# Opening of a two-block transformer kernel: who shifts the first chunk, which split comes first, and the order of the products

## The reference, cut to what matters

```
mods = silu(c) @ w_ada + b_ada            # 9 vectors of 1024: shift, scale, gate, three times
n = rmsnorm(x, g_pre) * (1 + scale) + shift
f = (silu(n @ w_gate) * (n @ w_up)) @ w_down
```

## Time and profile before

| | |
|---|---|
| median of three runs | 1135.86 us |
| the profiled execution | 1135.31 us |
| its span, first to last instruction | 1134.0 us |
| TensorE busy | 1118.3 us, 99% |
| VectorE busy | 821.5 us, 72% |
| ScalarE busy | 637.4 us, 56% |
| GpSimd busy | 56.6 us, 5% |
| granted TensorE clock | 0.999 of full |

### The profile page before, as it was taken

One profiled execution on the slowest core, in us unless ns is written; L12 is line 12 of the kernel. 1 busy time (PEld: TensorE's weight loads), 2 busy tenths in 40 slices (PEclk: granted clock), 3 DMA queues, 4 the chain that ended last, 5 costly groups with the idle time before them and its releaser, 6 DMA issues.

```text
span 1134.0 us, 16844 instructions
## 1 busy us (share of the span) xinstructions
PE 1118.3 (99%) x6542; PEld 979.6 (86%) x6542; DVE 821.5 (72%) x1416; ACT 637.4 (56%) x1203; POOL 56.6 (5%) x68
## 2 busy tenths in 40 slices
PE   8999999999999999999999999999999999999997
PEld 6998989799987888888899988888889988888886
DVE  6998788798666766676777867766667866766665
ACT  6664354856746655555765546555456654555553
POOL 2200000000001000000012300000000100000000
PEclk9999999999999999999999999999999999999999
DMA  9989999684232666668453336555554434655530
GB/s 385 420 314 383 298 389 261 233 337 159 98 112 75 231 219 208 238 223 191 147 202 112 112 112 223 186 186 188 188 182 162 173 107 150 213 190 191 193 128 37
DMA packets 36992, 231.10 MB, mean 204 GB/s; under 512 B 6825, under 2 KB 8241, under 8 KB 9522
## 3 DMA queue, kind: packets, MB, share of 16 engines
q1 hardware_dynamic: 31536, 225.59, 56.4%
q10 hardware_dynamic: 5378, 4.45, 1.3%
HBM read 228.95 MB, written 1.07 MB: 203 GB/s over the span
## 4 chain that ended last, share of the span: by engine, by line
PE 87%; DVE 5%; ACT 4%; DMA 2%; issue 1%; POOL 1%; ACTq 0%; DVEq 0%; POOLq 0%
PE ps L1718 43%; PE pacc L1718 42%; ACT whi L1998 1%; DVE wlo L2270 1%; DMA raw<-in_stream 1%; ACT arena L2105 1%; DMA cl<-in_cols 1%; POOL st L2600 1%; ACT wk L2208 0%; PE ps L1857 0%; PE ps L1928 0%; DVE wlo L2280 0%; ACT arena L1998 0%; DVE st L2495 0%; DVE h L2386 0%
## 5 line engine op out<-in xcount | busy, mean ns | idle before, releaser
L2270 DVE TENSOR_TENSOR wlo<-raw,whi 128x1024 fp32r<-128x1024 f32 x346 | 414.9, 1223 | 115.3 <-ACT whi L1998 114.8
L1718 PE MATMUL ps<-both,whi 128*128 128x256 f32 (+2 forms) x1728 | 460.6, 339 | 1.9 <-ACT both L1998 1.0
L1998 ACT ACTIVATE whi<-raw 128x1024 fp32r<-128x1024 f32 x346 | 360.4, 1056 | 98.4 <-PE ps L1718 44.1
L1718 PE MATMUL ps<-both,wlo 128*128 128x256 f32 x1264 | 354.6, 281 | 0.0
L1718 PEld LDWEIGHTS ps<-both,whi 128*128 128x128 f32 (+1 forms) x1728 | 296.7, 189 | 42.3 <-issue 3.7
L1718 PEld LDWEIGHTS ps<-both,wlo 128*128 128x128 f32 x1264 | 238.8, 189 | 2.9
L1718 PE MATMUL pacc<-whi,both 128*128 128x512 f32 (+2 forms) x352 | 106.5, 383 | 1.2 <-ACT both L2121 0.6
L1998 ACT ACTIVATE sg<-ps 128x256 f32<-128x256 f32 (+1 forms) x98 | 37.3, 380 | 100.3 <-PE ps L1718 100.1
L2290 DVE SCALAR_TENSOR_TENSOR raw<-raw,silu_c 128x1024 f32<-128x1024 f32 x72 | 89.8, 1255 | 3.6 <-DMA raw<-in_stream 3.6
L1718 PE MATMUL pacc<-whi,mhi 128*128 128x512 f32 x228 | 90.7, 398 | 0.0
L1718 PE MATMUL pacc<-whi,mlo 128*128 128x512 f32 x228 | 89.4, 392 | 0.0
(11 more groups left out here) (280 smaller groups left out, 1470.3 us busy)
## 6 DMA issues: line engine op xcount, KB each, us to landing
raw<-in_stream SPq DMA_DIRECT2D x213, 1024.0 KB, 5.0
gates<-gate_rows ACTq DMA_DIRECT2D x3, 512.0 KB, 7.4
h<-in_x SPq DMA_DIRECT2D x2, 512.0 KB, 4.4
cst<-in_const ACTq DMA_DIRECT2D x1, 1024.0 KB, 4.7
arena<-bias_rows ACTq DMA_DIRECT2D x1, 1024.0 KB, 28.6
arena<-in_final_g SPq DMA_DIRECT2D x1, 512.0 KB, 5.8
out<-tmp SPq DMA_DIRECT2D x2, 256.0 KB, 2.0
out<-tmp ACTq DMA_DIRECT2D x2, 256.0 KB, 2.3
```

The costliest lines, as they stand in the source:

```text
L1718: return e.matmul(o, a, b, start=start, stop=stop)
L1998: return e.activation(o, a, ACT.Copy, **how)
L2270: return e.tensor_tensor(o, a, hi.bitcast(F32), ALU.subtract)
```

## The change

Three edits, all in the opening.

1. For k = 0 the shift and scale of the chunk move from ACT to DVE: a new step `first_shifted` reads PSUM and writes `zs`. It stands behind the columns and ahead of `feed(3)`. ACT's part of `first_chunk` for k = 0 is then only the copy to `nhi`.
2. The last `feed` of iteration k stops one unit earlier, at 4k+7. The split of the second unit `fu` of chunk k+1 is thereby added by `feed(4(k+1)+4)`, behind the columns and the first chunk of k+1. On ACT the order becomes: copy of `fg`, columns, shift, copy to `nhi`, copy of `fu`. On DVE it becomes: two `ada` units, subtraction of `fg` (then `nlo`, where DVE makes it), subtraction of `fu`, the next two `ada` units. Iteration 7 still ends with `feed(34)`.
3. For k = 1 to 6 the 48 matmuls go in two groups of eight blocks (all gate blocks, then all up blocks): eight high by high, eight with the weights' low part, eight with the chunk's low part. For k = 0 the order stays.

```diff
+        z = tick("z0")
         if k == 0:
+            add("first_shifted", src=zs[0][0:2], full=zs[0][3], cols=t_cols)
             feed(3)
...
-        feed(4 * k + 8 if k < 7 else 34)
+        feed(4 * k + 7 if k < 7 else 34)
...
-            for four in range(4):
-                some = st.order[4 * four:4 * four + 4]
-                passes = [(p, jn) for jn in some for p in ((0, 0), (1, 0), (0, 1))]
-                if st.k == 0:
-                    passes = [(p, jn) for p in ((0, 0), (0, 1), (1, 0)) for jn in some]
-                for n, ((a, c), (j, u)) in enumerate(passes):
+            some, kinds = (4, ((0, 0), (0, 1), (1, 0))) if st.k == 0 else (8, ((0, 0), (1, 0), (0, 1)))
+            for at in range(0, 16, some):
+                group = st.order[at:at + some]
+                for n, ((a, c), (j, u)) in enumerate([(p, jn) for p in kinds for jn in group]):
...
-            src = m.bank(st.src[0])[:, st.src[1]:st.src[1] + T] if k == 0 else z
-            q.wait_ge(*st.full)
-            q.wait_ge(*st.cols)
-            e.activation(z, src, ACT.Identity, bias=m.mod[:, 8 + k:9 + k], scale=m.mod[:, k:k + 1]).then_inc(S["z0"], 1)
+            if k:
+                q.wait_ge(*st.full)
+                q.wait_ge(*st.cols)
+                e.activation(z, z, ACT.Identity, bias=m.mod[:, 8 + k:9 + k], scale=m.mod[:, k:k + 1]).then_inc(S["z0"], 1)
             q.wait_ge(*st.z)
             copy(m.nhi[:, k, :], z).then_inc(S["nhi"], 1)
...
+        elif kind == "first_shifted":
+            q.wait_ge(*st.full)
+            q.wait_ge(*st.cols)
+            b, at = st.src
+            e.tensor_scalar(m.zs[:, 0, :], m.bank(b)[:, at:at + T], m.mod[:, 0:1], m.mod[:, 8:9], ALU.mult,
+                            ALU.add).then_inc(S["z0"], 1)
```

More of the change, by code:

```diff
@@ L932, in schedule @@
         hi, lo = tick("nhi"), tick("nlo" if lane == "dve" else "nlo_p")
-        add("first_chunk", k=k, src=zs[k][0:2] if k == 0 else None, full=zs[k][3], cols=t_cols, z=tick("z0"), hi=hi, lane=lane)
+        add("first_chunk", k=k, full=zs[k][3], cols=t_cols, z=z, hi=hi, lane=lane)
         n1.t[k] = [hi, lo]
@@ L1762, in tensor_program @@
                     t = mul(m.bank(st.banks[j])[:, u * T:(u + 1) * T], m.unit(w, j * P, (j + 1) * P)[a], x[c], first)
-                    if n == 11 and (j, u) == [jn for jn in st.order if jn[1] == u][-1]:
+                    if n == 3 * some - 1 and (j, u) == [jn for jn in st.order if jn[1] == u][-1]:
                         t.then_inc(S["used"], 1)
```

## The result

The change made the kernel slower by about what was forecast. The median of 12 runs is 1138.13 us (1137.42 to 1140.24), against 1135.78 for 12 runs of the kernel before beside them: a ratio of 1.0018, interval 1.0009 to 1.0026. The medians lie 2.35 us apart; the ratio, which is not that of the medians, stands for 2.0 us. The interval leaves out 1, and eleven of the twelve runs before (up to 1137.02) are faster than every run after. The forecast was 1137.7. The profiled execution took 1138.04 us, its span is 1136.7 us, its granted clock 0.998.

The account below looks back on a forecast made before the run. TensorE, busy 99% of the span, was taken as the bound. Waits won (1.27 us) against five rounds of 6.04 instead of 5.76 (1.4) and chunk 7's late `fu` (1.8): net 1.8 slower, median 1137.7, range 1136.9 to 1138.6.

Parts of the forecast that it names:

- The circle: Chunks 2 to 7: a chunk's sums wait, through the `fu` subtraction and ACT's `fu` copy, on the previous sums; 6.04 us.
- The round: Once through the circle, from one chunk's sums to the next chunk's: 6.04 us, against TensorE's 5.76 a chunk.
- ACT's half: From the sums' end through scale column, shift, `nhi` and `fu` copy to DVE's subtraction: 2.53 us.
- DVE's half: The `fu` subtraction (1.14 us), the next chunk's two sums (1.14 and 1.15) and reading the sum (0.08).
- Chunk 1 and chunk 2: TensorE's waits at these chunks go: chunk 1 wins 0.84 us, chunk 2's wait for POOL 0.43, together 1.27.
- the sum: Total of the opening's terms: 1.27 us won, 1.4 lost over five rounds, 1.8 for chunk 7's late `fu`; net 1.8 slower.
- The end of chunk 7: Chunk 7's late `fu` subtraction holds its fifth matmul until 57.7; TensorE ends at 63.1 instead of 61.29, 1.8 us late.
- Behind the down rows: Hidden blocks' chain and weight subtraction after the opening: they move about as much as TensorE; price 0, up to 0.3 us.
- Rival 1: POOL's subtraction takes 1.71 us beside DVE, adding 0.52 to each of five rounds: 2.6 us, median 1140.3; chance 0.12.
- Rival 2: Rounds of 5.4 us or less, so TensorE never waits and 1.4 us are won: 1134.5; chance 0.12.
- break-even: Round of 5.67 us, where chunk 7's sums end at 52.0 and its `fu` is just in time for 61.29.
- Rival 3: Slack behind the opening catches the delay up later: 1135.9 us; chance 0.08.

Follow-up runs that it names:

- e3: Changed kernel, but on DVE the `fu` subtraction of chunks 1 to 6 goes behind both next sums; 1134.22 us, ratio 0.9993 to the kernel before.
- e6: Changed kernel with ACT's copy to `nhi` made twice for chunks 1 to 7; 1140.86 us, ratio 1.0048 to the kernel before.
- e2: Kernel before with edit 2 alone; 1138.40 us, ratio 1.0028 to the kernel before.
- e10: Kernel before with edit 3 alone; 1134.55 us, ratio 0.9986 to the kernel before.
- e5: Changed kernel, but chunk 7's `fu` is split ahead of its columns, as before; 1136.59 us, ratio 1.0009 to the kernel before.
- e1: Changed kernel with edit 2 taken back, leaving edits 1 and 3; 1134.61 us, ratio 0.9994 to the kernel before.
- e4: Changed kernel with edit 2 kept for chunk 1 only; 1134.65 us, ratio 0.9995 to the kernel before.
- e9: The kernel of e3, unchanged, timed a second time; 1135.12 us, ratio 0.9995 to the kernel before.
- e8: The kernel of e3 without edit 1, so ACT shifts chunk 0 as before; 1134.57 us, ratio 0.9991 to the kernel before.
- e7: Kernel before with ACT's copy to `nhi` made twice for chunks 1 to 7; 1135.80 us, ratio 1.0002 to the kernel before.

## Why the prediction was right

**The circle.** Every link was where the prediction put it: ACT behind the sums, DVE behind the copy of `fu`, the sums behind the subtraction. The round was forecast at 6.04 and came at 6.07, and e3 (cut it and the loss goes, with the same instructions) and e6 (lengthen it and each round grows) show that it is the cause; e2 shows that edit 2 suffices for it. Of the round's 0.03 above the forecast all lies in ACT's half: 2.56 from the sums' end to the subtraction (30.17 to 32.73), forecast 2.53, where the step from DVE to ACT, put at 0.03 without a row, took 0.04. DVE's half took 3.51, as forecast.

**Chunk 1 and chunk 2** lost their waits, as forecast (the sum put chunk 2's at 0.43; with the slow matmuls behind it, it was worth the 0.53 that e10 shows), and that lead was used up by the circle: chunk 7 begins at 56.15, before at 55.53.

**The end of chunk 7.** The fifth matmul was forecast at 57.7 and came at 58.26, for `wlo`. e5 puts the price of this step alone at 1.1 to 1.3 us. It is less than the 1.8 of the sum, because without it TensorE meets the next wait, for the low part of chunk 7, 0.47 us long.

**The size.** The down rows came at 63.63, not 63.1. Of the 0.5 the largest part is the start: the columns of chunk 0 were ready at 12.39 (0.22 from 12.17), not 11.94, because in this execution the opening's first loads landed later (TensorE's first work, which waits for one, starts at 3.01, in the kernel before at 2.18), as they also did in some of the others, with and without edit 1. This share is the chance of an execution and no part of the mechanism. That gives 0.43 at the end of the first pair of sums (17.99, forecast 17.56). Six rounds of 6.07 add 0.19, and the end of chunk 7 took 0.1 less than forecast. Behind the down rows the sum said 0, up to 0.3: the next block came 0.17 late (5.64 after the down rows, before 5.47, from the rows at 69.27 and 63.63), and some 0.2 more are spread over the rest and were not placed. So the profiled execution took 1138.04 instead of 1137.1.

**Edit 1** was costed at a new instruction of 0.43, from the one row of its kind. It took 0.55 (DVE's timeline, kernel after):

```profile
12.17 0.22 DVE L2319 SCALAR_TENSOR_TENSOR mod<-adac,cl,mod 128x1 f32<-128x1 f32 x1
12.50 0.55 DVE L2325 TENSOR_SCALAR wk<-pacc,mod 128x256 f32<-128x256 f32 x1
12.96 1.22 DVE L2270 TENSOR_TENSOR wlo<-raw,whi 128x1024 fp32r<-128x1024 f32 x1
```

That is under the 0.56 from which the prediction had it hold up the subtraction behind it, but the 0.56 counts from columns that are ready at 11.94. Here they came at 12.39, while ACT's copy of `fg` was done at 12.46, and the subtraction began only at 12.96, behind the new instruction. So the edit was not free: chunk 0's low part came at 14.51 (before 14.12), its fifth matmul at 14.56, and the chunk ended at 19.94 instead of the forecast 19.6. e1, e4 and e5 show the same hold; e3 and e9, with earlier columns or a later copy, do not. The circle hid this step's failure, since from chunk 3 on the sums set the pace. The new instruction scales and shifts by two columns, the rows of line 2267 only scale; whether that makes it longer no run shows. Counted from the columns, the first pair of sums came 0.38 us earlier than before (5.60 after them, before 5.98); forecast was 0.36.

**Rival 1** fell: all five of POOL's subtractions took 0.74 in DVE's wait, and from chunk 1 on no sum was longer than 1.22. The Trainium skill's rule on the shared port ("SBUF — State Buffer", "Who interferes with whom") agrees with both sides: in e1, where POOL starts at 31.14 while DVE's sum from 30.82 runs, POOL's row and the DVE sum behind that one are long again.

```profile
31.14 1.50 POOL L2620 TENSOR_TENSOR both<-wk,both 128x256 fp32r<-128x256 f32 x1 [5.17 <-ACT both L1998]
```

```profile
30.82 1.22 DVE L2290 SCALAR_TENSOR_TENSOR raw<-raw,silu_c 128x1024 f32<-128x1024 f32 x1
...
31.96 1.75 DVE L2290 SCALAR_TENSOR_TENSOR raw<-raw,silu_c 128x1024 f32<-128x1024 f32 x1
```

**Rival 2** asked for a round of 5.4 or less; it was 6.07. Its break-even of 5.67 counts five rounds from 23.61; the sums make six from 17.56, which gives 5.74, and 6.07 is over either. It names what e3 then built: with the links open, DVE's own 4.6 a chunk leaves TensorE its 5.76. **Rival 3** fell: from the down row to the end it is 1072.7 to 1073.1 us in every kernel here but e2 (1073.5), whether the row is at 59.81 or at 66.15. So no delay is caught up; the three slowest (the kernel after, e2 and e6) lose a further 0.3 to 0.8 behind it.

## What to carry to other kernels

When work is moved later in one engine's list, look at what stands behind it in the lists of the engines that wait for it: here a copy that TensorE did not need early stood, through DVE's order, in front of sums that ACT needed for its next copy, and two engines that were each busy for less than a chunk's time were tied into a loop longer than it. Such a loop shows before the change is built: follow the waits and the program order from one instruction to the same one of the next round, add the start-to-start times, and compare with the engine that should set the pace. If it is too long, changing the order at one link can be enough; nothing has to become faster.

## What was not expected of the hardware

The first matmuls of chunk 0 run at one of two paces, and the pace changes where the full clock begins. In e8 the first eight take 1.18 us from the first start to the next group's (13.33 to 14.51), and in the kernel before as much. In e3 they take 1.84 (13.21 to 15.05). TensorE's timeline of e3, then of e8:

```profile
13.21 2.00 PE L1720 MATMUL ps<-both,whi 128*128 128x256 f32 x8 [0.26 <-ACT both L1998]
15.05 0.64 PE L1720 MATMUL ps<-both,wlo 128*128 128x256 f32 x4
...
19.84 0.64 PE L1720 MATMUL pacc<-both,whi 128*128 128x256 f32 x4
```

```profile
13.33 1.34 PE L1718 MATMUL ps<-both,whi 128*128 128x256 f32 x8 [0.47 <-ACT both L1996]
14.51 0.64 PE L1718 MATMUL ps<-both,wlo 128*128 128x256 f32 x4
...
19.45 0.71 PE L1718 MATMUL pacc<-both,whi 128*128 128x256 f32 x4
```

Taken one by one from e3's trace, the starts are 13.21, 13.56, 13.77, 13.99, 14.20, 14.52, 14.73, 14.93, 15.05 and 15.17. They are 0.21 apart up to 14.93, but for the first and the fifth gap (0.35 and 0.32), and 0.12 from there. The trace lists the granted clock by stretches, and in e3 the first one listed, at full speed, begins at 14.89. For the time before it nothing is listed, and the view of windows counts such time as full. So the 1.00 in this row of e3 is no reading of the clock (busy time by engine, clock, DMA share, GB/s):

```profile
13.50:14.00 0.50, 0.50 (x4) 0.50 (x3) 0.50 (x2) 0.50 (x2) 0.00 (x0) 1.00 0.93 393
```

In e4, e9 and e10 the first listed stretch begins at 14.93, 15.32 and 14.82, and there too the starts are some 0.21 apart before it and 0.12 behind it. In e5 and e7 it begins at 13.79 and 13.88, and only the first gap of chunk 0 is long (0.34). In e8, in the kernel before and in the kernel after it begins ahead of chunk 0, at 12.64, 12.03 and 13.46, and the matmuls are 0.12 apart from the second on, but for the wait at the fifth. That the clock stood at the lower of its two levels before is read from the pace, since it is not listed. The Trainium skill ("TensorE: Matmul & The Clock Gate", Part 1) gives a matmul's start-to-start time as its columns over the clock; an estimate from it for 256 columns is 0.21 us at the lower of the two levels, 1.2 GHz. The 0.21 of e3, e4, e9 and e10 agrees.

Chunk 1 begins 0.4 to 0.8 later in e3, e4 and e9 (19.84, 20.00 and 20.22) than in e8 (19.45). The fifth matmul, the first to read the low part, follows the end of that part by 0.05 to 0.12 in all four. From it to the ninth they take 0.85, 0.75 and 0.96, and e8 0.58. So 0.2 to 0.4 of the difference goes with the slow pace; the low part itself came later too (14.09, 14.34 and 14.39, in e8 13.88). In e10 the slow start cost nothing, as chunk 1 waits for its high part in any case. The medians are of executions of which one alone has a trace, so how much of the smaller gains of e4 and e9 is the clock's is not shown. Nor is it shown why the full clock begins at 12.0 in one execution and at 15.3 in another.
